# Two-layer hybrid attention block: the values of a whole group of four units in one visit to the array's column mode

## The reference

```python
def block(args):                                   # MLA: 8 heads, query blocks of 128
    logits = jnp.einsum('bqhd,bkhd->bhqk', qi, k) * scale
    p = masked_softmax(logits, kpos[None, :] <= qpos[:, None])
    return jnp.einsum('bhqk,bkhd->bqhd', p.astype(v.dtype), v)
...
# NSA: 8 heads in 2 groups, three branches (compressed, selected, window)
o_slc = jnp.einsum('bghqn,bgqnd->bqghd', ps.astype(v_sel.dtype), v_sel)
o_win = jnp.einsum('bghqk,bkgd->bqghd', pw.astype(vw.dtype), vw)
o = gi[..., 0:1] * o_cmp + gi[..., 1:2] * o_slc + gi[..., 2:3] * o_win
```

## Time and profile before

| | us |
|---|---|
| median of three runs | 1303.52 |
| lowest, highest | 1303.19, 1304.73 |
| profiled execution | 1304.81 |
| its span, first to last instruction | 1303.0 |
| PE busy | 1265.0 (97%) |
| VectorE busy | 704.0 (54%) |
| ScalarE busy | 639.2 (49%) |
| PE's wait list, attention copies (L871 and L878) | 11.9 in 16 waits |

### The profile page before, as it was taken

How to read it: one execution, slowest core, us unless ns; L and a number is a source line. 1 busy time by engine, 2 the same in 40 slices (tenths; PEclk the granted TensorE clock), 3 DMA queues, 4 the chain that set the end, 5 groups by cost and what they waited for, 6 DMA issues and landing times.

```text
span 1303.0 us, 18497 instructions
## 1 busy us (share of the span) xinstructions
PE 1265.0 (97%) x6612; PEld 1045.6 (80%) x6612; DVE 704.0 (54%) x1232; ACT 639.2 (49%) x1193; POOL 71.1 (5%) x157
## 2 busy tenths in 40 slices
PE   8999989999999999999999998999999999999997
PEld 7997667778888888888889876677888888888885
DVE  5435887454555555533363459872555555554334
ACT  4336888344444444322352479881444444443223
POOL 2003020000000000000010311100000000000000
PEclk9999999999999999999999999999999999999999
DMA  6420200123333333332143211002233333333221
GB/s 206 125 90 1 98 34 1 39 73 113 95 93 100 95 93 102 103 97 96 53 122 95 65 66 50 17 1 81 81 85 95 97 97 95 96 101 108 97 64 65
DMA packets 121002, 107.04 MB, mean 82 GB/s; under 512 B 3763, under 2 KB 110485, under 8 KB 120946
## 3 DMA queue, kind: packets, MB, share of 16 engines
q1 hardware_dynamic: 118912, 101.13, 25.3%
q0 software_dynamic: 1456, 3.52, 0.9%
q10 hardware_dynamic: 578, 1.64, 0.3%
HBM read 104.19 MB, written 2.10 MB: 82 GB/s over the span
## 4 chain that ended last, share of the span: by engine, by line
PE 84%; DVE 8%; ACT 6%; issue 2%; DMA 0%; ACTq 0%; DVEq 0%
PE ps L1449 24%; PE ps L1451 24%; PE ps L1450 24%; PE ps L1692 3%; PE ps L1645 3%; DVE probs L1184 2%; ACT probs L860 2%; PE ps L1626 1%; PE ps L1632 1%; DVE w_lo L577 1%; PE ps L1631 1%; DVE probs L1057 1%; DVE x L1075 1%; PE ps L1704 1%; DVE ht_lo L1064 1%
## 5 line engine op out<-in xcount | busy, mean ns | idle before, releaser
L1449 PE MATMUL ps<-ht_hi,w_hi 128*128 128x512 f32 (+2 forms) x776 | 298.2, 384 | 2.5 <-DVE w_lo L577 2.5
L1450 PE MATMUL ps<-ht_lo,w_hi 128*128 128x512 f32 (+2 forms) x776 | 296.9, 383 | 0.0
L1451 PE MATMUL ps<-ht_hi,w_lo 128*128 128x512 f32 (+2 forms) x776 | 296.8, 382 | 0.0
L577 DVE TENSOR_TENSOR w_lo<-raw,w_hi 128x1024 fp32r<-128x1024 f32 (+4 forms) x196 | 219.8, 1146 | 96.0 <-ACT w_hi L570 86.9
L570 ACT ACTIVATE w_hi<-raw 128x1024 fp32r<-128x1024 f32 (+4 forms) x196 | 187.2, 983 | 108.0 <-PE ps L1451 107.1
L1365 DVE SCALAR_TENSOR_TENSOR conv<-ps,cols,conv 128x510 f32<-128x510 f32 (+1 forms) x176 | 127.6, 746 | 181.4 <-ACT conv L969 175.6
L1449 PEld LDWEIGHTS ps<-ht_hi,w_hi 128*128 128x128 f32 x776 | 146.4, 189 | 30.8 <-DVE w_lo L577 3.0
L1450 PEld LDWEIGHTS ps<-ht_lo,w_hi 128*128 128x128 f32 x776 | 146.5, 189 | 28.0 <-issue 0.5
L1451 PEld LDWEIGHTS ps<-ht_hi,w_lo 128*128 128x128 f32 x776 | 146.5, 189 | 27.8
L1449 PE MATMUL ps<-w_hi,ht_hi 128*128 128x430 f32 (+1 forms) x392 | 147.4, 376 | 2.6 <-DVE w_lo L577 1.5
L969 ACT ACTIVATE conv<-ps,cols 128x512 f32<-128x512 f32 x88 | 68.1, 773 | 160.0 <-PE ps L1451 159.8
(11 more groups left out here) (200 smaller groups left out, 1508.5 us busy)
## 6 DMA issues: line engine op xcount, KB each, us to landing
raw<-in_ffn_w_up_dram SPq DMA_DIRECT2D x88, 512.0 KB, 4.4
raw<-in_ffn_w_down_dram SPq DMA_DIRECT2D x44, 512.0 KB, 3.3
raw<-in_w_in_dram SPq DMA_DIRECT2D x32, 430.0 KB, 4.4
raw<-in_w_out_dram SPq DMA_DIRECT2D x16, 512.0 KB, 3.7
raw<-in_nsa_cmp_w_dram SPq DMA_DIRECT2D x8, 512.0 KB, 3.7
x<-in_x_dram ACTq DMA_DIRECT2D x3, 512.0 KB, 7.7
raw<-in_mla_w_uq_dram SPq DMA_DIRECT2D x4, 384.0 KB, 2.9
out_dram<-x SPq DMA_DIRECT2D x3, 512.0 KB, 2.6
```

The costliest lines, as they stand in the source:

```text
L577: last = nc.vector.tensor_tensor(d(w_lo)[:, :, d0:d1], r(raw)[:, :, r0:r1], d(w_hi)[:, :, d0:d1].bitcast(F32), ALU.subtract)
L1449: mm(o, lhs[0], rhs[0], start=start, stop=False)
L1450: mm(o, lhs[0], rhs[1], start=False, stop=False)
L1451: return mm(o, lhs[1], rhs[0], start=False, stop=stop)
```

## The change

The values of a group's big units no longer follow two steps after their transposes in a visit of their own. They are multiplied in the step in which the small units' values are, ahead of these, in one visit: 24 matmuls in the trace (28 with the compressed branch) instead of 16 and 8. The big units' probabilities must therefore be kept longer. The two tiles of pts become pt_big, with three places of one query block each (two that take turns for block 2, one for block 3), and pt_small for blocks 0 and 1; together they are as large as before. The block 2 of the next group is copied while the old one's values are still to come, which is why it has two places. The three conditions on which copies wait are counted anew: block 3 waits for the big values of the group before, block 2 for those two groups before, the small ones for the small values of the group before.

```diff
--- before.py
+++ after.py
@@ -266,7 +266,8 @@
         w_lo = sb("w_lo", [P, SLOTS, 1024], F32R)
 
         probs = sb("probs", [P, 3, 2, S])
-        pts = [sb(f"probs_t{n}", [P, 2, T, 2 * P]) for n in range(2)]
+        pt_big = sb("probs_t_big", [P, 3, 2, T, P])
+        pt_small = sb("probs_t_small", [P, 2, 2, 2 * P])
         ident = sb("ident", [P, P])
         causal = sb("causal", [P, S])
         table = sb("table", [P, S])
@@ -316,8 +317,8 @@
         silu = sb("silu", [P, 2, S], F32, ffn)
         ffn.close()
 
-        kpe_r = pts[1][:, 0, :, 0:2 * ROPE].rearrange("p t (a b) -> p t a b", a=2)
-        rows = pts[0][:, 0, :, :].rearrange("p a (b c) -> p (a b) c", c=P)
+        kpe_r = pt_small.rearrange("p a t c -> p (a t) c")[:, :, 0:2 * ROPE].rearrange("p t (a b) -> p t a b", a=2)
+        rows = pt_big[:, 0, :, :, :].rearrange("p a b c -> p (a b) c")
         hn = probs[:, 0:2, :, :].rearrange("p s a n -> p s (a n)")
         norm_g = probs[:, 2, :, :].rearrange("p a n -> p (a n)")
 
@@ -591,9 +592,23 @@
             n -= U_MLA // T
             return i, H // 2 + n // 2, n % 2
 
-        def pt_half(u):
-
-            return pts[(u // 2) % 2]
+        def pt_unit(u):
+
+            i = unit(u)[0]
+            if i == T - 1:
+                return pt_big[:, 2, :, :, :]
+            if big(u):
+                return pt_big[:, u // T % 2, :, :, :]
+            return pt_small[:, :, :, i * P:(i + 1) * P]
+
+        def pt_pair(u, h, b):
+
+            if not big(u):
+                return pt_small[:, h, b, b // (half_blocks(u) - 1) * P:2 * P]
+            if b == T - 1:
+                return pt_big[:, 2, h, b, :]
+            first = u // T % 2
+            return pt_big[:, first::2 - first, h, b, :]
 
         def half_blocks(u):
 
@@ -862,20 +877,24 @@
 
                 def evac_turn(u):
 
-                    blocks, q = unit(u)[0] + 1, unit(u)[0] % 2 * P
+                    blocks, g = unit(u)[0] + 1, u // T
                     act.wait_ge(t_done, at(t_done, l, turns(u, 0)))
-                    if u >= T:
-                        act.wait_ge(pv_done, at(pv_done, l, u // 2 - 1))
+                    if not big(u) and g >= 1:
+                        act.wait_ge(pv_done, at(pv_done, l, 2 * g))
+                    elif unit(u)[0] == T - 1 and g >= 1:
+                        act.wait_ge(pv_done, at(pv_done, l, 2 * g - 1))
+                    elif g >= 2:
+                        act.wait_ge(pv_done, at(pv_done, l, 2 * g - 3))
                     bank = TURN_BANK[u, 0][0]
                     if big(u):
-                        activate(pt_half(u)[:, 0, 0:blocks, q:q + P],
+                        activate(pt_unit(u)[:, 0, 0:blocks, :],
                                  ps[:, bank, 0:blocks * P].rearrange("p (b q) -> p b q", q=P), ACT.Copy).then_inc(pt_act, 1)
                         act.wait_ge(t_done, at(t_done, l, turns(u, 1)))
-                        activate(pt_half(u)[:, 1, 0:blocks, q:q + P],
+                        activate(pt_unit(u)[:, 1, 0:blocks, :],
                                  ps[:, TURN_BANK[u, 1][0], 0:blocks * P].rearrange("p (b q) -> p b q", q=P), ACT.Copy)\
                             .then_inc(pt_second, 1)
                     else:
-                        activate(pt_half(u)[:, :, 0:blocks, q:q + P],
+                        activate(pt_unit(u)[:, :, 0:blocks, :],
                                  ps[:, bank, 0:2 * blocks * P].rearrange("p (a b q) -> p a b q", a=2, q=P), ACT.Copy)\
                             .then_inc(pt_act, 1)
 
@@ -1690,7 +1709,7 @@
                                 c = COL_KV + (branch + 1) * 2 * G * HD + G * HD + r // 2 * HD
                                 w = proj[:, b, c:c + HD]
                             last = mm(ps[64 * h:64 * h + VD, out_bank(g), q0 + q:q0 + 2 * P], w,
-                                      pt_half(u)[:, h, b, q:2 * P], start=b == 0, stop=b == n - 1)
+                                      pt_pair(u, h, b), start=b == 0, stop=b == n - 1)
                     last.then_inc(pv_done, 1)
 
                 def compressed(r):
@@ -1783,7 +1802,8 @@
                         pe.wait_ge(k_ready, at(k_ready, l, H // 2))
                     if s >= LAG + U_MLA and (s - LAG - U_MLA) % (2 * T) == 2 * T - 1:
                         compressed((s - LAG - U_MLA) // (2 * T))
-                    if s >= LAG and s % 2 == 1:
+                    if s >= LAG and (s - LAG) % T == T - 1:
+                        values(s - LAG - 2)
                         values(s - LAG)
                     if s >= U and s - U < FILL:
                         pe.wait_ge(max_done, at(max_done, l, 2 * U))
```

## The result

The changed kernel takes 1338.08 us, the median of six runs (1336.25 to 1342.68), against 1304.12 for six runs of the kernel before beside it: a ratio of 1.0264 (1.0251 to 1.0277). It is slower by 34 us. The forecast was 1330, with a range of 1315 to 1341.

The account below looks back on a forecast made before the run. It took TensorE, busy for 97% of the span, and its waits to bound the kernel. 1304.81 + 23.0 (groups) + 3.4 (clock) = 1331.2 profiled, 1329.9 on the median, stated as 1330; range 1315 to 1341, own range 1320 to 1336.

Parts of the forecast that it names:

- The cover: Before the spread: without the visit, PE waits for VectorE's factors, 1.0 us in groups 7, 9, 1.8 in 6, 8, 10.
- Removed and added: Each group on PE: visit removed 1.78 us, merged matmuls added 1.52; 0.26 saved if PE never waited.
- rival A: The factors are ready in time in all 24 groups: 6.2 us faster, 1297.3 us; chance 0.06.
- Groups 6 to 10: Attention groups: 1.52 us lost in each of 6, 8, 10 and 0.76 in 7, 9; 6.08 us a layer.
- Groups 0 to 5: Early attention groups, which wait already: lateness adds up, less what idle times give back, to 5.92 us a layer.
- Group 4's give-back of 1.08: Group 4: VectorE's late third-block row maximum gives back 1.08 us, leaving 2.98 of 4.06 us lateness before the added 1.52.
- The conditions and buffers: ScalarE's three new copy conditions and the operands' new strides: they cost nothing.
- The clock: PE's waits in groups 2 to 5: 2 of 8 possible falls to half clock, 1.7 us each, 3.4 us.
- B: Groups 0 to 5 absorb the moved work, only later groups lose: 1314.7 us; chance 0.14.
- C: Clock falls in each of groups 2 to 5 of both layers, 8 x 1.7 us: 1340.1 us; chance 0.14.

Follow-up runs that it names:

- e5_norm: Changed kernel with VectorE's output normalization and addition moved ahead of block 2's row maxima; 1325.34 us, ratio 1.0159.
- e6_norm_fac: As e5_norm, and from group 6 on VectorE's factors also stand ahead of block 3's row maxima; 1321.11 us, ratio 1.0114.
- e9_late_only: Changed kernel with merged visit, early normalization and early factors from group 6 on only, groups 0 to 5 as before; 1301.17 us, ratio 0.9973.
- e8_before_norm: Kernel before the change, with only VectorE's normalization and addition moved ahead of block 2's row maxima, no values moved; 1306.55 us, ratio 1.0019.
- e4_buffers: Changed kernel's new buffers and conditions alone, with the big values back in their old separate visit; 1304.77 us, ratio 0.9999.
- e3_early: Changed kernel with values merged in groups 0 to 5 only, two visits in groups 6 to 11; 1326.01 us, ratio 1.0154.
- e1_fill: Changed kernel with block 0's score matmuls done four extra times in groups 1 to 4, filling TensorE's waits; 1332.45 us, ratio 1.0203.
- e2_late: Changed kernel with values merged in groups 6 to 11 only, two visits in groups 0 to 5; 1316.49 us, ratio 1.0087.

## Why the prediction came out as it did

Direction and mechanism held; of the sum, one term was mis-sized. The result lies inside the range of 1315 to 1341 but near its upper end, and outside the narrower 1320 to 1336 that the forecast was given for itself.

**The cover (held).** The 1.78 us that the visit took between the fourth block's scores and the spread were the cover of VectorE's factors. After, the spread comes at t0 + 6.15 and + 5.35 in turn (forecast 6.15 and 5.35), and e5_norm and e6_norm_fac show the cause: with VectorE's order changed and PE's left alone, the wait shrinks and goes. The waits were put at 1.8 and 1.0; the rows show 1.69 and 0.89:

```profile
217.19 0.66 PE L1678 MATMUL ps<-ident,onorm 128*128 128x128 f32 x4 [0.89 <-DVE onorm L1218]
```

The bracket counts from the modelled end of the transposes (t0 + 4.46 in group 8), I had counted from when the spread's start would have been due (t0 + 4.33). The starts of the spread are those forecast, and the merged visit of group 8 lasts 2.39 us (228.78 to 231.17), forecast about 2.4.

**Removed and added (held behind a wait, a little off without one).** 1.78 out and 1.52 in were to give 0.26 for a visit. Where PE waits for the factors, 1.52 came in (groups 6 and 8). Where it does not, the spread of e9_late_only comes 1.81 earlier than before in group 7 (t0 + 4.30 for 6.11), and what follows it lasts 1.61 longer: 0.19 saved, not 0.26. Against e8_before_norm it is 0.19 in the even groups too. For rival A that means about 24 x 0.19 = 4.6 us instead of 6.2, an estimate from groups 6 to 10 alone.

**Groups 6 to 10 (held).** 1.52, 0.80, 1.52, 0.80, 1.19 = 5.83 a layer against 6.08. Most of the 0.33 less in group 10 is the wait of 0.25 at the earlier trace rows, which I had taken off group 11: it stands ahead of that group's t0. Group 11's small values start at 263.33 - 250.35 = t0 + 12.98, before at 246.84 - 233.56 = t0 + 13.28: 0.30 saved. Groups 10 and 11 together: forecast + 1.01, measured + 0.89.

**Groups 0 to 5 (held).** 5.92 forecast, 6.07 by the table's last column. Group 4's give-back of 1.08 from VectorE's late start came out as 1.13. In layer 2 group 0 gave back 0.33 less (16.94 without a fall, against 16.61). Both layers together: 23.5 us against 23.0.

**The conditions and buffers (held).** e4_buffers, 0.0 us.

**The clock (wrong in number).** The term that was mis-sized is "I take 2 falls of the 8 possible: 3.4 us". Seven falls at 1.6 us each are 11.2; the fall in the feed-forward net, which the time before contains, did not come (1.7 back): 9.5 instead of 3.4. With it: 1304.81 + 23.5 + 11.2 - 1.7 = 1337.8, against 1338.40 measured. The price of a fall was right (1.7 against 1.6, as group 10 at 9.53 and 11.12 shows), and the number of falls makes up 6.1 (9.5 less 3.4) of the 7.2 us between the sum for the profiled execution (1331.2) and its time (1338.40). Another 0.5 lies in the groups, and 0.6 is not accounted for.

Two things in the reasoning were wrong. I counted only groups 2 to 5 as possible places, as their waits grow to 2 to 3 us. But of the seven falls three stood elsewhere, in group 1, group 0 of layer 2 and group 10 of layer 2. The last of these had only the wait for the factors right before it:

```profile
905.62 1.00 PE L1678 MATMUL ps<-ident,onorm 128*128 128x128 f32 x4 [1.69 <-DVE onorm L1218]
```

And I took the 1.60 us wait at 178.57, after which the clock had stayed up, as a sign that waits of that size are safe. In group 4 it grew to 3.10, and the clock fell 0.6 us after its end:

```profile
185.01 0.52 PE L1664 MATMUL ps<-ident,probs 128*128 128x128 f32 x3 [3.10 <-ACT probs_t_small L897]
```

**The rivals.** A (1297.3) failed since the factors are not there at t0 + 4.33; where they were made to be there from group 6 on, a gain came, at 0.19 us a visit. B (1314.7) is refuted by e3_early. C (1340.1) named the right effect with a number of falls near the truth, but with the wrong places. Its total is the nearest of all to the result (2 us off); I had given it 0.14. That it is so near is in part luck, as only four of its eight falls stood where it has them.

**Open.** When exactly a wait brings the clock down is not settled. The wait of 1.69 us for the factors comes six times in the profiled execution, alike each time; once the clock fell behind it. In e1_fill it fell behind two of the six, both in group 6, and in e2_late behind one, in group 10 of layer 2 again. The runs of the changed kernel lie up to 6.4 us apart (1336.25 to 1342.68) and their mean granted clock goes with the time (0.991 for the shortest, 0.984 for the longest); 6.4 us is the size of four falls, but only one execution is profiled, so this is argued and not shown.

## What to carry to other kernels

Before a run of work is moved on the engine that bounds a kernel, look at what stands behind it there: if the next instruction waits for another engine and starts within the moved time of its release, the run was cover. Moving it then costs up to its whole length: here 1.52 us where nothing was in hand and 0.80 where the factors had been ready 0.8 us early, for a saving of 0.19. The repair is on the other engine: move what the waited-for result does not need into the idle time ahead of it, and only in those groups where that engine has such idle time. Where new waits come up on TensorE in a busy stretch, add to them the falls of its clock that they may bring, each at the price that a fall in the same trace shows, and count every such wait as a candidate, here from 1.69 us on.

## What was not expected of the hardware

A wait of 1.69 to 3.10 us in an else fully busy stretch of TensorE can bring 3.4 us at half clock and cost 1.6 us on top of itself; the seven of them together, 11.2 us, are a third of the 33.6 that the profiled execution lost. The same wait at the same place brings it in one layer and not in the other. And matmuls whose results are thrown away can pay for themselves: 26 us of them in the waits made the changed kernel 10 us faster (1338.1 to 1327.9), with no fall left in the attention stages. Whether they would win anything in the kernel before, whose waits are shorter, was not tried.
